# RWKV-7 recurrence in two lanes: token products behind levels 1 and 2 of a lane's inverse, the other lane's back-transposition and gate behind levels 2 and 3

## What is computed

```python
def step(S, inp):
    r_t, d_t, k_t, v_t, kk_t, b_t = inp
    sa = einsum('bhvk,bhk->bhv', S, kk_t)
    S = S * d_t - sa[..., None] * b_t + v_t[..., None] * k_t
    return S, einsum('bhvk,bhk->bhv', S, r_t)
# then: y normalised over a head's 64 values, scale and offset,
# plus bonus * v, times the gate g, and the product with wo
```

## Time and profile before

| | |
|---|---|
| median of the runs | 3231.15 us |
| profiled execution | 3231.09 us |
| span of its profile | 3229.6 us |
| TensorE busy | 3153.0 us, 98% |
| VectorE busy | 2085.2 us, 65% |
| ScalarE busy | 1405.4 us, 44% |

### The profile page before, as it was taken

One profiled execution on the slowest core, in us unless ns is written; L12 is line 12 of the kernel. 1 busy time (PEld: TensorE's weight loads), 2 busy tenths in 40 slices (PEclk: granted clock), 3 DMA queues, 4 the chain that ended last, 5 costly groups with the idle time before them and its releaser, 6 DMA issues.

```text
span 3229.6 us, 80506 instructions
## 1 busy us (share of the span) xinstructions
PE 3153.0 (98%) x31912; PEld 2959.4 (92%) x31912; DVE 2085.2 (65%) x3633; ACT 1405.4 (44%) x2321; POOL 128.8 (4%) x245
## 2 busy tenths in 40 slices
PE   7999999998999999999999999999999999999998
PEld 3799987777999999999999988998999999999998
DVE  3544546776568978778788866455589954445445
ACT  2433436665454534333344644334465544343442
POOL 0000000110000000000000000000000000000000
PEclk9999999999999999999999999999999999999999
DMA  9878750002878888878777532432457754445443
GB/s 396 331 269 295 275 193 23 22 22 90 316 284 301 298 310 301 311 291 306 267 240 254 192 117 95 144 131 92 162 197 241 245 172 163 167 163 165 163 163 120
DMA packets 182928, 668.83 MB, mean 207 GB/s; under 512 B 21366, under 2 KB 21536, under 8 KB 182208
## 3 DMA queue, kind: packets, MB, share of 16 engines
q1 hardware_dynamic: 155808, 570.43, 49.5%
q0 software_dynamic: 26912, 95.47, 9.0%
HBM read 661.73 MB, written 4.09 MB: 206 GB/s over the span
## 4 chain that ended last, share of the span: by engine, by line
PE 93%; DVE 3%; DMA 2%; issue 1%; ACT 1%; SPq 0%; DVEq 0%; ACTq 0%
PE ps L2171 52%; PE ps L2154 8%; PE ps L2156 7%; PE ps L2155 7%; PE ps L2332 5%; PE ps L2117 2%; DMA sb_raw<-stream 2%; PE ps L2128 1%; PE ps L2324 1%; PE ps L2649 1%; PE ps L2650 1%; PE ps L2651 1%; PE ps L2693 1%; PE ps L2692 1%; PE ps L2276 1%
## 5 line engine op out<-in xcount | busy, mean ns | idle before, releaser
L737 ACT ACTIVATE sb_whi<-sb_raw 128x1024 fp32r<-128x1024 f32 x778 | 811.3, 1057 | 1066.9 <-PE ps L2171 759.6
L1217 DVE TENSOR_TENSOR sb_wlo<-sb_raw,sb_whi 128x1024 fp32r<-128x1024 f32 x778 | 942.3, 1221 | 505.7 <-ACT sb_whi L737 503.2
L2171 PE MATMUL ps<-sb_ah,sb_whi 128*128 128x288 f32 (+1 forms) x2776 | 485.2, 297 | 0.0
L2171 PE MATMUL ps<-sb_al,sb_whi 128*128 128x288 f32 (+1 forms) x2776 | 483.3, 296 | 0.0
L2171 PE MATMUL ps<-sb_ah,sb_wlo 128*128 128x288 f32 (+1 forms) x2776 | 481.2, 295 | 0.0
L2171 PEld LDWEIGHTS ps<-sb_ah,sb_whi 128*128 128x128 f32 x2776 | 408.8, 189 | 7.8 <-issue 7.0
L2171 PEld LDWEIGHTS ps<-sb_al,sb_whi 128*128 128x128 f32 x2776 | 407.9, 189 | 0.0
L2171 PEld LDWEIGHTS ps<-sb_ah,sb_wlo 128*128 128x128 f32 x2776 | 407.2, 188 | 0.0
L2154 PE MATMUL ps<-sb_ah,sb_whi 128*128 128x288 f32 (+1 forms) x952 | 286.5, 301 | 0.7 <-DVE sb_x L1356 0.7
L2156 PE MATMUL ps<-sb_al,sb_whi 128*128 128x288 f32 (+1 forms) x952 | 283.2, 297 | 0.0
L2155 PE MATMUL ps<-sb_ah,sb_wlo 128*128 128x288 f32 (+1 forms) x952 | 282.5, 297 | 0.0
(11 more groups left out here) (338 smaller groups left out, 4547.2 us busy)
## 6 DMA issues: line engine op xcount, KB each, us to landing
sb_raw<-stream SPq DMA_DIRECT2D x1070, 512.0 KB, 4.5
sb_strip<-strips POOLq DMA_DIRECT2D x156, 512.0 KB, 5.1
sb_crow<-crow POOLq DMA_DIRECT2D x8, 512.0 KB, 5.4
sb_x<-xT SPq DMA_DIRECT2D x1, 2304.0 KB, 15.6
sb_x<-xT POOLq DMA_DIRECT2D x1, 2304.0 KB, 9.3
yT<-sb_x SPq DMA_DIRECT2D x4, 576.0 KB, 2.8
sb_lwa<-lw POOLq DMA_DIRECT2D x16, 130.0 KB, 2.4
sb_lwg<-lw POOLq DMA_DIRECT2D x16, 130.0 KB, 2.4
```

Source lines behind the costliest of these rows:

```text
L737: nc.scalar.activation(whi[:, q % SPL, :], raw[:, n, :], ACT.Copy).then_inc(hi_ready, 1)
L1217: nc.vector.tensor_tensor(wlo[:, q % SPL, :], raw[:, n, :], whi[:, q % SPL, :], ALU.subtract).then_inc(lo_ready, 1)
L2171: ins = mm(PS[:, m, 0:s.wide], w[:, n % SPL, a:a + P], z[:, 2 * p + j, 0:s.wide], start=False, stop=False)
```

## The change

Nothing is computed in another way; only the order of issue in `beside` changes, on three engines.

```diff
@@ ScalarE, beside
                     inverse(f, i, 1)
                     token(f, i, T_MV, t["km"][:, :, 1, :])
                     inverse(f, i, 2)
+                    token(f, i, T_B, t["ng"][:, :, 0, :])
+                    inverse(f, i, 3)
+                    token(f, i, T_K, t["kt"][:])
                 if g is not None:
                     back(g, j)
                 if f is not None:
-                    inverse(f, i, 3)
                     inverse(f, i, 4)
+                    inverse(f, i, 5)
                 if g is not None:
                     high(g, j)
-                if f is not None:
-                    token(f, i, T_B, t["ng"][:, :, 0, :])
-                    inverse(f, i, 5)
-                    token(f, i, T_K, t["kt"][:])
@@ VectorE, beside
                 if f is not None:
                     level(f, i, 3)
+                    level(f, i, 4)
                 if g is not None:
                     output(g, j)
                     gated(g, j)
-                if f is not None:
-                    level(f, i, 4)
-                if g is not None:
                     low(g, j)
@@ TensorE, beside
                     level(f, i, 0)
                     mixed(f, i)
                     level(f, i, 1)
+                    tokens_b(f, i)
+                    level(f, i, 2)
+                    tokens_k(f, i)
                 if g is not None:
                     back(g, j)
                 if f is not None:
-                    level(f, i, 2)
+                    level(f, i, 3)
                 if g is not None:
                     gate(g, j)
                 if f is not None:
-                    level(f, i, 3)
-                    tokens_b(f, i)
                     level(f, i, 4)
-                    tokens_k(f, i)
```

## The result

The changed kernel takes 3272.06 us (median of 4 runs, 3268.52 to 3277.31), the kernel before 3231.2 us. The ratio is 1.0125, with a 95% interval of 1.0113 to 1.0138. The profiled execution has a span of 3267.0 us, 37.4 more than before; it is the fastest of the four. Its TensorE clock is 0.991 over the span.

The account below looks back on a forecast made before the run. TensorE, busy 283.34 of 310 us in the recurrence, was taken to bound the kernel, so waits count. 3231.1 + 28.2 (latency) + 12.8 (clock falls) = 3272 us; range from 3251 to 3300 us.

Parts of the forecast that it names:

- Level 2 at 1.54, level 3 at 3.40, level 4 at 5.43, level 5 at 8.54 after level 1: Predicted TensorE start times in us within a round of the recurrence; level 5 came at 6.66 before, so +1.88 us.
- Level 4 to level 5 in 3.11 us: On ScalarE and VectorE: last yt copy, high, low and level 5's predicated copy run end to end, 0.98+0.31+0.54+0.75+0.53 us.
- Rival 4: Output's tail is off level 5's path: +0.31 us a round, +5 us, 3236 us; 3228 without stalls; chance 0.04.
- 28.2 us of latency in 15 rounds: Recurrence: level 5 comes 1.88 us later in each of 15 rounds, adding 28.2 us.
- rival 3: TensorE's issue stalls, 8.1 us over the recurrence, vanish in the gap ahead of level 5: 3251 us; chance 0.04.
- Falls of the clock in half of the rounds at 1.7 us, 12.8 us: TensorE's 2.25 us gap ahead of level 5 lowers its clock in half of the rounds: 7.5 x 1.7 = +12.8 us.
- Rival 1: TensorE's clock holds despite the gap, leaving only the added latency: 3259 us; chance 0.32.
- Rival 2: TensorE's clock falls in every round: 3285 us, with 3310 as the far end; chance 0.10.
- The sum: Whole kernel: 3231.1 + 28.2 latency + 12.8 clock = 3272 us, the forecast, chance 0.50.

Follow-up runs that it names:

- High first: Changed kernel with one swap on ScalarE: the output's rounding (high) ahead of the last yt copy instead of behind it; 3249.76 us, ratio 1.0052.
- low behind level 5: Changed kernel with one move on VectorE: the output's remainder (low) behind level 5's predicated copy instead of ahead of it; 3242.99 us, ratio 1.0035.
- filled version: Changed kernel with six matmuls of unused result added on TensorE behind level 4 in each of 15 rounds; 3257.08 us, ratio 1.008.
- VectorE's part undone: Changed kernel with output and gated put back ahead of level 4's predicated copy on VectorE; 3303.17 us, ratio 1.0227.
- VectorE's part alone: Kernel before with only VectorE's reordering: level 4's predicated copy ahead of output and gated; 3243.98 us, ratio 1.0037.

## Why the prediction was right, step by step

- **Level 2 at 1.54, level 3 at 3.40, level 4 at 5.43, level 5 at 8.54 after level 1.** Measured 1.53, 3.38, 5.41, 8.50. The costs read from one round of before (latency 1.54, tokens 0.34, `back` 0.66, gate 1.17) could be put together in a new order without loss.
- **Level 4 to level 5 in 3.11 us, because `high` stands behind the last yt copy and `low` ahead of level 5's copy.** Measured 3.09. High first and low behind level 5 each remove their link, and level 5 moves as the link says. Rival 4 is refuted by the chain of waits. Its size was too small: with the tail taken off the path the change is still slower, by 12 us and not by 5; 4 of the 7 us more are stalls of issue.
- **28.2 us of latency in 15 rounds.** In the round shown the stretch grew by 1.84 us, which makes 27.6 us. Of this about 23 us reached the time: the filled version, with the clock at 1.00, has rounds longer by 23.0 us in all. Its stalls of issue total 4.7 us instead of 8.1, which is 3.4 of the difference. So some of the stalls went, as in rival 3, but that the gap took them in, as that rival says, is not shown and is unlikely: VectorE's part undone has the same gap and a second one and 10.8 us of stalls, and VectorE's part alone has 4.7 us without any gap above 0.8.
- **Falls of the clock in half of the rounds at 1.7 us, 12.8 us.** Measured: 7 of 15 rounds, 1.7 us each by the mean of the rounds, 11 to 12.6 us by the gap-filled version. Both factors were hit by luck. The frequency was a choice between none and all. The price was half of what 6.8 us at the low clock could cost; a low stretch here is some 3.5 us long, and of the 1.75 us that it can cost 1.4 to 1.7 were paid. Rival 1 (3259) is what the filled version runs at, 3257. Rival 2 is not seen: the same gap of 2.17 us stands in every round (once 2.52), and the clock falls behind 8 of 15 gaps (behind the last one in the stretch that follows the 15 rounds). What decides between a gap with a fall and one without is not shown. That the falls differ from run to run fits the four runs of the changed kernel: their granted clocks over the span are 0.991, 0.990, 0.989 and 0.988, their times 3268.5, 3270.5, 3273.6 and 3277.3 us.
- **The sum.** 3272 against 3272.06 is closer than its terms. The profiled execution is 3231.1 + 23.0 (latency, net of stalls) + 12.6 (clock, with up to 1.5 of stalls) + 1.8 (outside the 15 rounds) = 3268.5. So the latency term was 5 us too high, and 1.8 us that the prediction did not have came outside the rounds; the median execution lies another 3.5 us above the profiled one.

## What to carry to other kernels

When a filler is moved from behind one step to behind another, look at what it leaves bare, and at what each engine's queue then has between the bare step and the next. A copy that nobody waits for becomes part of the critical path when it stands ahead of one that is waited for, and the cost is the sum of all such links. Here, on a TensorE that is nearly full, a recurring gap of 2.17 us cost more than the delay itself: some 11 us of falls of the clock came on top of 23 us.

## What was not expected of the hardware

- Six matmuls without use made the changed kernel 15 us faster, by keeping the granted clock at 1.00 instead of 0.96 in the rounds.
- The clock fell behind gaps as short as 1.5 us (high first: 0.99 over its rounds, with falls in two of them, each behind a round with over 2 us of stalls), and not in the rounds of the two kernels in which TensorE's idle time ahead of level 5 was 0.6 us (low behind level 5, gap filled). The Trainium skill ("TensorE: Matmul & The Clock Gate", section "HAM oscillation — how this bites in real kernels") has it fall in every turn of a loop whose bursts are parted by DMA waits of about 3 to 5 us. Those waits are longer than any gap here, so that loop is no measure for this one. Here, with gaps of 2.17 us and most of each round filled, it was 7 of 15 rounds.
- Stalls of issue on TensorE, in which it waits for nothing that the profile shows, are not a constant of the program: 8.1 us before, 6.2 in the changed kernel, 4.7 with the gap filled, 12 with low behind level 5, for nearly the same instructions. Their places go by the count of instructions rather than by time: in low behind level 5 and in VectorE's part undone the four rounds with the most of them (2.0 to 2.6 us each) are the 1st, 5th, 9th and 13th of the 15, though a round takes 20.5 us on average in the one and 24.6 in the other. Their cause stays open.
